# ScalarE instead of VectorE copies the first attention's numerators out of PSUM, and six more quads fold their probabilities before the transpose

## The reference

```python
logits = jnp.einsum('bdhnqc,bdhnkc->bdhnqk', qb, kb) * scale + bias[None, None, :, None]
logits = jnp.where(valid, logits, -jnp.inf)
m = jnp.max(logits, axis=-1)
p = jnp.exp(logits - m[..., None])
s = jnp.sum(p, axis=-1)
num = jnp.einsum('bdhnqk,bdhnkc->bdhnqc', p, vb)
...
m_all = jnp.max(jnp.stack(maxes), axis=0)
wts = [jnp.exp(mx - m_all) for mx in maxes]
num_tot = sum(w[..., None] * n for w, n in zip(wts, nums))
den_tot = sum(w * d for w, d in zip(wts, dens))
o_attn = (num_tot / den_tot[..., None]).reshape(B, S, ATTN_WIDTH).astype(x.dtype)
```

## Time and profile before

| | |
|---|---|
| median of 3 runs | 2543.37 us (2543.09 to 2543.72) |
| the profiled execution, its own time | 2550.03 us |
| its span in the trace | 2548.2 us |
| mean granted TensorE clock | 0.994 |
| PE busy | 2496.3 us (98%) |
| DVE busy | 1438.6 us (56%) |
| ACT busy | 1062.9 us (42%) |

### The profile page before, as it was taken

One profiled execution on the slowest core, in us unless ns is written; L12 is line 12 of the kernel. 1 busy time (PEld: TensorE's weight loads), 2 busy tenths in 40 slices (PEclk: granted clock), 3 DMA queues, 4 the chain that ended last, 5 costly groups with the idle time before them and its releaser, 6 DMA issues.

```text
span 2548.2 us, 41821 instructions
## 1 busy us (share of the span) xinstructions
PE 2496.3 (98%) x15772; PEld 2018.4 (79%) x15772; DVE 1438.6 (56%) x2729; ACT 1062.9 (42%) x2118; POOL 1140.3 (45%) x1390
## 2 busy tenths in 40 slices
PE   7999999999999999999999999999999999999999
PEld 6887777777777777777788888788888888777787
DVE  4006465465866657576541777766668005588843
ACT  4124546555433333142112553555555113477731
POOL 3332233233433233231356736577777455444452
PEclk9999999999999999999999999999999998999999
DMA  4241221211201111011432323333335114201132
GB/s 143 84 132 46 66 60 54 74 52 42 67 19 54 39 34 52 26 55 68 164 127 65 106 98 98 110 100 100 101 104 193 44 48 141 67 26 35 34 116 83
DMA packets 234440, 198.96 MB, mean 78 GB/s; under 512 B 7296, under 2 KB 202240, under 8 KB 233728
## 3 DMA queue, kind: packets, MB, share of 16 engines
q1 hardware_dynamic: 188800, 120.60, 15.7%
q10 hardware_dynamic: 45440, 75.68, 8.3%
HBM read 150.64 MB, written 45.61 MB: 77 GB/s over the span
## 4 chain that ended last, share of the span: by engine, by line
PE 85%; DVE 8%; ACT 4%; POOL 1%; issue 1%; DMA 0%; ACTq 0%; SPq 0%; DVEq 0%; POOLq 0%
PE gemm L831 15%; PE gemm L833 14%; PE gemm L832 14%; PE gemm L1294 5%; PE gemm L1296 5%; PE gemm L1295 5%; PE scores L903 2%; PE weighted L933 1%; PE scores L1498 1%; PE weighted L1521 1%; PE scores L1372 1%; PE probs_t L1165 1%; PE probs_t L918 1%; PE scores L1069 1%; PE scores L1169 1%
## 5 line engine op out<-in xcount | busy, mean ns | idle before, releaser
L781 POOL CAST w_hi<-w_raw 128x512 fp32r<-128x512 f32 x264 | 197.8, 749 | 1151.6 <-PE gemm L833 1012.7
L783 POOL TENSOR_TENSOR w_lo<-w_raw,w_hi 128x256 fp32r<-128x256 f32 x528 | 446.1, 845 | 41.7
L831 PE MATMUL gemm<-h_hi,w_hi 128*128 128x512 f32 x1072 | 449.6, 419 | 1.3 <-DVE h_lo L2026 1.3
L833 PE MATMUL gemm<-h_hi,w_lo 128*128 128x512 f32 x1072 | 420.3, 392 | 0.0
L832 PE MATMUL gemm<-h_lo,w_hi 128*128 128x512 f32 x1072 | 419.0, 391 | 0.0
L831 PEld LDWEIGHTS gemm<-h_hi,w_hi 128*128 128x128 f32 x1072 | 202.3, 189 | 48.5 <-issue 14.3
L833 PEld LDWEIGHTS gemm<-h_hi,w_lo 128*128 128x128 f32 x1072 | 201.3, 188 | 44.1
L832 PEld LDWEIGHTS gemm<-h_lo,w_hi 128*128 128x128 f32 x1072 | 202.5, 189 | 32.3 <-issue 1.7
L1642 DVE CUSTOM_DVE_ANT_0 neg_logits<-scores,bias_tile 128x128 f32<-128x128 f32 (+1 forms) x192 | 67.7, 352 | 254.0 <-PE scores L903 239.6
L2545 ACT ACTIVATE prob<-neg_logits,row_max 128x128 f32<-128x128 f32 (+1 forms) x192 | 86.8, 452 | 128.5 <-DVE row_max L1642 109.1
L831 PE MATMUL gemm<-xn_hi,w_hi 128*128 128x512 f32 x288 | 118.1, 410 | 2.0 <-DVE xn_lo L2297 1.8
(11 more groups left out here) (647 smaller groups left out, 6209.5 us busy)
## 6 DMA issues: line engine op xcount, KB each, us to landing
w_raw<-in_w_in SPq DMA_DIRECT2D x73, 512.0 KB, 3.9
w_raw<-in_a_w_in SPq DMA_DIRECT2D x28, 512.0 KB, 4.1
w_raw_b<-in_a_w_in SPq DMA_DIRECT2D x20, 512.0 KB, 4.7
gates_scratch<-o_f ACTq DMA_DIRECT2D x32, 256.0 KB, 2.0
merge_gates<-gates_scratch ACTq DMA_DIRECT2D x4, 2048.0 KB, 10.4
mlp_v_scratch<-v_piece ACTq DMA_DIRECT2D x32, 256.0 KB, 2.0
mlp_v<-mlp_v_scratch ACTq DMA_DIRECT2D x16, 512.0 KB, 4.2
w_raw<-in_a_w_out SPq DMA_DIRECT2D x16, 512.0 KB, 4.1
```

What stands on the lines that cost most here:

```text
L781: Q(pool.tensor_copy(weight_part(u, 0, ks), raw[:, s, ks, :]))
L783: Q(pool.tensor_tensor(weight_part(u, 1, ks), raw[:, s, ks, :], weight_part(u, 0, ks).bitcast(F32), ALU.subtract), E("w_split") if ks.stop ...
L831: pe.matmul(dst, w_high, hi(k, h), start=first, stop=False)
L833: m = pe.matmul(dst, w_low, hi(k, h), start=False, stop=last)
```

## The change

`collect` moves from DVE's list to ACT's, where it is the first compute step of a slot, ahead of `copy_back`. It becomes an activation (Copy) of the same tile, and takes its waits with it. DVE's `blend` waits in addition for the last `pv_free` of the pass. `folds(c)` is now true also for quads 4 and 5 of passes 1, 2 and 3 (group 1, t = 0 and 1): six quads more. These lose `copy_back` on ACT (two activations each), get `fold` and `parted` on DVE, and have 4 transposes instead of 6.

```diff
@@ -488,7 +488,7 @@
         def folds(c):
 
             p, g, t = quads[c]
-            return g < 2 and (p == 0 or not 2 <= 4 * g + t <= 5)
+            return g < 2 and (p == 0 or not 2 <= 4 * g + t <= 3)
@@ -1643,17 +1643,6 @@
-            def collect(c):
-
-                p, g, t = quads[c]
-                dve.wait_ge(E("pv_full"), c + 1)
...
-                V(v.tensor_copy(natural(numer[p % 2][:, g:g + 1, :], g, t), permuted(PV[:, 0:256].unsqueeze(1), g)), E("pv_free"))
@@ -1716,6 +1705,7 @@
                 num = numer[p % 2]
+                dve.wait_ge(E("pv_free"), 12 * p + 12)
                 dve.wait_ge(E("w_spread"), 6 * p + b + 1)
@@ -1741,8 +1731,6 @@
                     biased(slot_of[s])
-                if s - 3 in slot_of:
-                    collect(slot_of[s - 3])
                 if s - 1 in slot_of and folds(slot_of[s - 1]):
@@ -2533,6 +2521,17 @@
+            def collect(c):
+
+                p, g, t = quads[c]
+                act.wait_ge(E("pv_full"), c + 1)
+                if c == 12:
+                    for n in range(8):
+                        act.wait_ge(E(f"load_{n}"), 64)
+                if c % 12 == 0 and p >= 2:
+                    act.wait_ge(E("oa_out_v_out2"), 16 * (p - 1))
+                A(a.activation(natural(numer[p % 2][:, g:g + 1, :], g, t), permuted(PV[:, 0:256].unsqueeze(1), g), ACT.Copy), E("pv_free"))
@@ -2610,6 +2609,8 @@
                     attn_out(oa_slots[s])
+                if s - 3 in slot_of:
+                    collect(slot_of[s - 3])
                 if s - 2 in slot_of and not folds(slot_of[s - 2]):
                     copy_back(slot_of[s - 2])
```

## The result

The changed kernel takes 2550.1 us (median of 11 runs, 2549.04 to 2550.88) against 2543.51 for the one before (11 runs on the same chip, 2542.58 to 2543.86): +6.6 us, a ratio of 1.0026 with a 95% interval of 1.0017 to 1.0034. The forecast was +3.4 us with a range up to 2550.5, so the time lies at the range's upper end, and on the side "slower by over 0.2%", to which I had given 0.18.

A forecast was written before the change was run, and what follows sets the result against it. PE was taken to bound the attention, busy 444.84 of 450.00 us. Copies at four places +5.4, numerators off DVE -0.7 and folds -1.3 gave +3.4 us: a median of 2546.8 us, range 2544.0 to 2550.5.

The forecast's parts named there:

- The copy's price: A strided numerator copy of groups 1 and 2 on ACT takes about 0.67 us, bounds 0.40 to 1.14.
- rival B: Numerator copies on ACT cost only what a contiguous copy does, 0.40 us each: +1.2 us, 2544.6; chance 0.14.
- rival A: Strided copy is dear on 128 partitions, over 0.89 us each, lengthening the row copies' wait: 2550.5 us; chance 0.15.
- The three first scores: First scores of passes 1 to 3 wait for two more ACT copies each: 3 x 2 x 0.67 = 4.0 us.
- Pass 0 and the folds: Transposes' waits for a fold in pass 0 go, -0.7 us; six more folds shorten twelve transposes, -1.3 us.
- rival E: Folds come late from DVE's load, PE waits six times for 0.5 us or more: 2549.8 or later; chance 0.05.
- C: Rival: the copies hide at the four places, only -2.0 us is left, 2541.4; chance 0.08.
- D: Rival: relief of DVE gives PE more than 5.1 us; chance 0.03.
- The fourth place: After the last pass, two more ACT copies delay DVE, then the weights PE waits for: another 1.3 us.

The follow-up runs named there:

- e5: Kernel before the change with only quads 4 and 5 of passes 1 to 3 folded, all numerators still on VectorE: 2542.78 us against 2543.86.
- d3: Kernel before the change with two more ScalarE statistics copies in the last pass only, ahead of VectorE's row work: 2546.11 us, ratio 1.0008.
- p1: Changed kernel with most GpSimd casts and subtractions left out for the two weight units between 625 and 650 us: 2548.68 us.
- e1: Changed kernel with the numerators of quads 9 and 10 of every pass copied by VectorE again: 2542.6 us, ratio 0.9993 to the kernel before.
- f1: e1 with the fourth group of statistics copies also moved from ScalarE to VectorE: 2539.23 us, ratio 0.9979 to the kernel before the change.

## Why the prediction was right or wrong

**The copy's price: right.** 0.67 us was taken; the copies of groups 1 and 2 have 0.63 to 0.70, those of group 0, contiguous, 0.384 at the least. That the row copy on 2 partitions set the price for 128 held. The Trainium skill's rule that the prediction quotes, 0.40 us, held for the contiguous ones only, so rival B falls, and so does rival A, which wanted 0.89.

**The three first scores: right as waits.** 6.8 us and 2.4 at the worst were named and came. The steps are 1.34, 1.3 (2.90 less the stretch) and 1.29 us, 3.9 in all for 4.0.

**Pass 0 and the folds: right.** -0.75 for -0.7, and -1.3 for -1.3, and e5 parts the two. No fold was late (rival E falls), the copies did not hide (C), and DVE's relief gave no more than the waits of pass 0 (D).

**The fourth place: the mechanism right, the size wrong.** The step that failed is "From there the chain goes through DVE to the weights, and PE waits for them as it is: another 1.3 us". The chain is that one, but its links were priced at their durations of before. They depend on what runs on GpSimd when they start, and the delay shifts that. It measured 2.40 us: DVE starts 1.46 later (4.85 less the 3.39 of shift that was there already), and the four operations take 8.26 us instead of 7.35, 0.91 more. ACT was late in one more place that I had taken as idle, the gemm's wait of 0.4 us, which costs nothing of its own, since PE waits for the weights behind it. d3 gives the same from a delay alone, and with most of GpSimd's work gone (p1) the excess is gone too. Rows of before could have warned: operations of one shape stand there with 1.75, 1.90 and 1.95 us, and the first of them has 2.05 in each of the passes before.

**The clock: not in the sum at all.** I took "all of it counts: 3 x 2 x 0.67" and read the wait as idle time alone. Waits of 2.0 to 2.4 us brought 1.2 GHz after them in 9 of 15 cases, 1.6 us each, so 1.6 to 3.2 us for the three places (one stretch in one profile of the changed kernel, two in the other); waits up to 1.1 us in none of 17. Without this term the time would have stayed within 0.2%.

**The sum.** -0.75 + 3.93 - 1.3 + 2.4 = +4.3 us without the clock. With one stretch it is 5.9, as in the first profile (5.79 + 0.08), with two 7.5, as in the second (7.69 - 0.19). The timed +6.6 lies between. The range held it, by luck, because it was opened to 9.1 us by a bound on the copy's price, a cause that didn't occur. That the time came near rival A's 2550.5 is a coincidence, since the copy has 0.64 us.

What stays open: what decides whether the clock falls behind a given wait, and what sets the low-clock stretches after 1200 us. In e1's profile they take back 1.2 us of its gain, which fits its median, but they vary from profile to profile, and no run separates them.

## What to carry to other kernels

Before moving work onto an engine because it has idle time on average, look for the places where another engine waits for it, and leave those places out: with ten of twelve copies moved (and the folds) PE gained 2.1 us up to the merge in the trace; with all twelve the trace has a loss of 5.9 us at that point (a second profile 7.5) and the timing one of 6.6. A wait of TensorE that grows from one microsecond to over two can cost more than itself, since the clock may fall behind it. The better kernel here came from taking work off such places (f1, 4.6 us under the kernel before, with the folds), until another engine's list became the late one. A chain of VectorE operations with two SBUF inputs has no fixed length while GpSimd works beside it.

## What the runs showed of the hardware that I had not expected

- At the first scores of a pass, after a wait of 2.0 to 2.4 us PE ran at 1.2 GHz for 3.4 us in 9 of 15 cases, at 1.6 us each, after 3.1 to 3.6 us in 4 of 4, and after up to 1.1 us in none of 17, in places that change from one execution of the same program to the next.
- VectorE's operation on 34 x 1536 elements takes 1.75 us alone and up to 2.23 beside GpSimd: 1.61 us plus the rest of the GpSimd instruction under way. A GpSimd cast of 0.61 us takes 2.03 behind it.
- A ScalarE copy of 256 elements from PSUM to a strided place has 0.62 to 0.70 us on 128 partitions and 0.61 to 0.70 on 2, against 0.384 contiguous.
